# Gated delta rule in blocks of 128 tokens instead of 64, inside a two-layer encoder kernel

## The chip, the cores and the metric

One core of one Trainium2 chip runs the whole program. The metric is the device time of one execution in microseconds (us). Three runs of the kernel before took 2283.44, 2287.17 and 2287.83 us (median 2287.17).

## What is computed

Two encoder layers on a 256 x 2048 input, in float32. Layer 0 is a mixer (half A: gated delta rule, 8 heads of 128; half B: a spatial gating MLP), layer 1 a convolution module, and each layer ends with a squared-ReLU MLP. The change is in half A alone, the gated delta rule. Cut to what matters:

```python
g = jnp.cumsum(g, axis=-1)                       # within each chunk
decay = jnp.exp(jnp.where(tri, g[..., :, None] - g[..., None, :], -jnp.inf))
a = jnp.where(strict, jnp.einsum("bhnid,bhnjd->bhnij", k_beta, k) * decay, 0.0) + eye
sol = triangular_solve(a, [v_beta, k_beta * exp(g)])   # u and w
attn = jnp.einsum("bhnid,bhnjd->bhnij", q, k) * decay
q_dec, k_tail, g_last = q * exp(g), k * exp(g_end - g), exp(g_end)
# scan over chunks, state starts at zero
v_new = u_c - w_c @ state
o_c = qd_c @ state + attn_c @ v_new
state = state * gl_c + kt_c.T @ v_new
```

The reference cuts the 256 tokens into chunks of 64. The result is the same, up to rounding, for any chunk length: the chunk length is only a way to order the work.

## The kernel before, in words

**Main stream.** Weights come in chunks of 1 MB (`raw`, SP queue, L224), are split into a high part by ACT (`high_part`, L278) and a low part by DVE (`low_part`, L579), and PE multiplies. In layer 0's projections PE works by `narrow_group` (L992): one group G is 16 steps, called quarters here (`advance(st, 16 * G + 2 * i + k)`, L1014), of 12 matmuls each (L1005, L1007, L1009). Four halves of two quarters are buffered (`SPLIT = 4`).

**Side streams.** The mixer's work is written as Python generators for PE, ACT and DVE, woven by hand into the main stream. A generator yields the number of the quarter at which its next step is due. PE calls them after each quarter's 12 matmuls, so a step is put into PE's program at the end of its quarter. ACT and DVE call them once per two quarters (`side_work`, L289 and L590), right after the high or the low part that becomes possible when PE has finished the odd quarter before: work due at an even quarter or the odd one behind it is done in the same call. All three engines run in program order, so a wait in a side step also holds up the main stream behind it.

**Mixer A** (PE L1119, ACT L386, DVE L721) works on four blocks b = 2 * hh + m, of four heads (hh) and 128 tokens (m) each. Block b starts at quarter 59 + 33 * b (`BLOCK_START`, `BLOCK_TIME`), so blocks 0 and 2 start at an odd quarter, 1 and 3 at an even one. The offsets in a block are in `AT` (L35): `tok` transposes q, k, v; `gb` the decays; `feat` and `attn` the products of keys and queries; then the inverse of the unit triangular matrix C by doubling. Level lev of `LEVELS = 5` is: PE y = C * T (L1156), DVE masks it into Z (L767), PE Z * U and U * Z (L1161, L1163), DVE copies U (L770), ACT copies T (L415). One level takes two quarters; the last one leaves out U * Z. The 128-token block holds two chunks of 64, so the inverse is block diagonal. Then w (L1167) and, for each chunk cc, a step v (L1174, L1175) and a step s (L1180, L1181 and the new state L1183) with a state update on DVE (L778, L781). The head norm follows (ACT L426, L428, DVE L784 to L787), then a transpose on PE at offset `o` (L1187) and the gate (L792, L796).

**Mixer B** (DVE L799, PE L1189) has four parts at quarters 144, 160, 176 and 192; its PE steps are L1200 and L1206. After the last block of A, POOL loads x again (2 MB, L258), which ACT (L461) and DVE (L842) wait for at the first group of the output projection.

A float32 product of one head (128 x 128) is two matmul entries in the trace, a transpose is one.

Of the kernel before, what the change touches and what calls it, by code (L numbers as in the profile page):

```python
# [34 lines left out]
AT = {"tok": 0, "gb": 8, "feat": 10, "attn": 12, "t_prod": 14, "levels": 15, "w": 25, "chunks": 26, "o": 31}  # L35
# [6 lines left out]
LEVELS = 5  # L42


CONSTS = ["ident", "ones", "upto", "chunk", "fill", "strict", "lev0t"] + [f"lev{i}" for i in range(1, LEVELS + 1)]

# [17 lines left out]
def build(nc, xt, wts, w_ba, consts, params, conv_w, dw, rows, w_s, out):  # L64
    with ExitStack() as ctx:
# [34 lines left out]
        def const(name):  # L100
            return ct[:, CONSTS.index(name), :]

# [16 lines left out]
        def all_heads(ap):  # L119
# [30 lines left out]
            "tok", "tok_sq", "ss", "root", "normed", "q_decayed", "lg", "gb", "elast", "kb_copy", "decay_in", "decay",  # L150
# [18 lines left out]
        for later, first in (("sq_k", "knT"), ("sq_q", "kbT"), ("C", "kn"), ("U", "qn"), ("T", "kb"), ("Z", "knT"),  # L169
                             ("wT", "kbT"), ("v_new", "qnT"), ("state_d", "decay_s"), ("o_sq", "decay"), ("o_n", "kd"),  # L170
                             ("gate_out", "kt")):
            buf[later] = buf[first]
# [4 lines left out]
        elast = small[:, 0:4].rearrange("p a m h -> p (a m h)")[:, 0:8].rearrange("p (h c) -> p h c", c=2)  # L177
# [89 lines left out]
        def _(act):  # L267
# [118 lines left out]
            def mixer_a():  # L386
                for b in range(4):
# [13 lines left out]
                    nc.scalar.activation(elast, bank(4)[:, :, C - 1::C], ACT.Exp).then_inc(s["elast"], 1)  # L401
# [6 lines left out]
                    copy(buf["qdT"], bank(5)).then_inc(s["feat_act"], 1)  # L408
# [7 lines left out]
                    yield start + AT["w"] + 1  # L416
                    act.wait_ge(s["w_prod"], b + 1)
                    nc.scalar.activation(buf["wT"], bank(6), ACT.Copy, scale=-1.0).then_inc(s["w_copy"], 1)
                    for cc in range(2):
                        R = slice(C * cc, C * cc + C)  # L420
                        yield start + AT["chunks"] + 2 * cc + 1
                        act.wait_ge(s["v_prod"], 2 * b + cc + 1)
                        copy(buf["v_new"][R], bank(6)[R]).then_inc(s["v_copy"], 1)
                    yield start + AT["chunks"] + 4
                    act.wait_ge(s["s_prod"], 2 * b + 2)
# [138 lines left out]
        def _(dve):  # L564
# [156 lines left out]
            def mixer_a():  # L721
                for b in range(4):
# [21 lines left out]
                    tt(buf["qd"], buf["qn"], per_head(eg), ALU.mult).then_inc(s["q_decayed"], 1)  # L744
                    tt(buf["kt"], buf["kn"], per_head(et), ALU.mult)

                    yield start + AT["gb"] + 1
                    dve.wait_ge(s["elast"], b + 1)
# [3 lines left out]
                    dve.wait_ge(s["normed"], b + 1)  # L752
                    tt(buf["kd"], buf["kb"], per_head(eg), ALU.mult)
# [10 lines left out]
                    for lev in range(1, LEVELS + 1):  # L764
                        yield start + AT["levels"] + 2 * lev - 1
                        dve.wait_ge(s["y_prod"], LEVELS * b + lev)
                        tt(buf["Z"], bank(6), all_heads(const(f"lev{lev}")), ALU.mult).then_inc(s["z"], 1)  # L767
                        yield start + AT["levels"] + 2 * lev
                        dve.wait_ge(s["ut_prod"], LEVELS * b + lev)
                        nc.vector.tensor_copy(buf["U"], bank(4)).then_inc(s["u_copy"], 1)  # L770
                    if m == 0:
                        if b:
                            dve.wait_ge(s["state"], 5 * hh)
                        nc.vector.memset(buf["state"], 0.0).then_inc(s["state"], 1)
                    for cc in range(2):
                        if m == 0 or cc == 1:
                            dve.wait_ge(s["state"], 5 * hh + 2 * m + cc + 1)
                        link(tt(buf["state_d"], buf["state"], elast[:, :, cc].unsqueeze(2).to_broadcast([P, HH, P]), ALU.mult))  # L778
                        yield start + AT["chunks"] + 2 * cc + 2
                        dve.wait_ge(s["s_prod"], 2 * b + cc + 1)  # L780
                        tt(buf["state"], bank(5), buf["state_d"], ALU.add).then_inc(s["state"], 1)  # L781

# [206 lines left out]
        def _(pe):  # L989
# [108 lines left out]
            def decay_products():  # L1098

                yield GATES_START + 14  # L1100
                pe.wait_ge(s["g"], 1)
                mm(ps[:, 6, 0:16], const("upto"), gates[:, 1].rearrange("p m h -> p (m h)"), start=True, stop=True)
                mm(ps[:, 6, 16:32], const("chunk"), gates[:, 1].rearrange("p m h -> p (m h)"), start=True,
                   stop=True).then_inc(s["gc_prod"], 1)
# [13 lines left out]

            def mixer_a():  # L1119
                for b in range(4):  # L1120
# [4 lines left out]
                    if b:  # L1125
                        pe.wait_ge(s["gated"], b)
                        pe.wait_ge(s["state"], 5 * ((b - 1) // 2) + 2 * ((b - 1) % 2) + 3)
                    else:
                        pe.wait_ge(s["g"], 2)
# [12 lines left out]
                    transposes(5, lambda h: buf["qd"][:, h, :])  # L1142
                    products(6, buf["knT"], buf["kbT"]).then_inc(s["feat"], 1)
                    yield start + AT["attn"]
                    pe.wait_ge(s["feat_act"], 2 * b + 2)
# [138 lines left out]
def tables():  # L1284
# [3 lines left out]
    same = i[:, None] // C == i[None, :] // C  # L1288
    upto = same & (i[:, None] <= i[None, :])
    t = {"ident": np.eye(P), "ones": np.ones((P, P)), "upto": upto, "chunk": same,  # L1290
# [72 lines left out]
```

## Time and profile before

| | before |
|---|---|
| median of 3 runs | 2287.17 us |
| the profiled execution, its own time | 2285.45 us |
| its span, first to last instruction | 2283.5 us |
| PE busy | 2198.2 us, 14110 matmuls |
| DVE busy | 1562.1 us, 1809 instructions |
| ACT busy | 972.6 us, 1042 instructions |
| mean granted TensorE clock | 0.989 |

The span is 1.95 us shorter than the execution's own time. Matmuls are pipelined: the duration of one is about 0.28 us while the next starts 0.11 us behind it, so the time of a step is read from the starts. The mixer A work lies between 118 and 455 us of the span.

### The profile page before, as it was taken

Reading aid. Unit: us, or ns where it says so; the run is one execution under the profiler, and the core shown is the slowest. Engines: PE = TensorE matmul, PEld = TensorE weight load, DVE = VectorE, ACT = ScalarE, POOL = GpSimd, SP = SyncE. Lnnn points to the kernel's source line nnn. Section 1 sums busy time; section 2 is a strip of 40 time slices with the busy share of each in tenths; the row PEclk is TensorE's granted clock in tenths of the full one; section 3 lists DMA queues with packets and bytes.
Section 4 is the critical chain, followed back from the end, with each engine's and each line's share of the span. In section 5 each row is a group of like instructions: output and inputs, shape, how many; then the busy total and the mean of one; then the engine's idle time right before and its main releaser. Section 6 shows DMA issues by size and latency. Waiting matters only on the chain.

```text
span 2283.5 us, 36015 instructions
## 1 busy us (share of the span) xinstructions
PE 2198.2 (96%) x14110; PEld 2023.7 (89%) x14110; DVE 1562.1 (68%) x1809; ACT 972.6 (43%) x1042; POOL 11.5 (1%) x25
## 2 busy tenths in 40 slices
PE   7999999889999999999999999899999999999996
PEld 7988898889999999999999888788899999999995
DVE  8676567467765765765674999977665665665765
ACT  4544344344444544544442100155444444444553
POOL 0000000000000000000000000000000000000000
PEclk9999999999999999999999999999999999999998
DMA  6432233255555555555554444244555555555553
GB/s 226 178 112 91 98 123 121 84 193 185 202 204 202 198 193 211 197 198 197 203 201 148 151 158 153 76 163 167 203 199 198 192 206 200 201 202 202 199 192 123
DMA packets 55864, 396.84 MB, mean 174 GB/s; under 512 B 6497, under 2 KB 6881, under 8 KB 8545
## 3 DMA queue, kind: packets, MB, share of 16 engines
q1 hardware_dynamic: 54288, 389.32, 47.0%
q0 software_dynamic: 1488, 6.29, 1.0%
q8 instruction: 63, 1.03, 0.2%
q14 instruction: 25, 0.20, 0.0%
HBM read 393.49 MB, written 2.10 MB: 173 GB/s over the span
## 4 chain that ended last, share of the span: by engine, by line
PE 77%; DVE 14%; issue 4%; ACT 3%; DMA 2%; DVEq 0%; ACTq 0%; SPq 0%; POOL 0%
PE ps L1030 40%; PE ps L1032 20%; DVE work L925 4%; PE ps L1057 4%; DVE wlo L579 3%; PE ps L1005 3%; PE ps L1007 3%; PE ps L1009 3%; PE ps L1116 2%; DMA raw<-in_wts 1%; ACT whi L278 1%; DVE sq_part L619 1%; PE ps L1181 1%; PE ps L1180 1%; DVE work L686 0%
## 5 line engine op out<-in xcount | busy, mean ns | idle before, releaser
L579 DVE TENSOR_TENSOR wlo<-raw,whi 128x1024 fp32r<-128x1024 f32 x672 | 817.3, 1224 | 493.4 <-ACT whi L278 479.6
L278 ACT ACTIVATE whi<-raw 128x1024 fp32r<-128x1024 f32 x672 | 705.9, 1057 | 714.3 <-PE ps L1032 362.2
L1030 PE MATMUL ps<-hid,whi 128*128 128x512 f32 x2304 | 755.7, 382 | 5.8 <-DVE hid L958 3.3
L1030 PE MATMUL ps<-xg,whi 128*128 128x512 f32 x2048 | 672.0, 382 | 7.1 <-ACT sq_part L323 4.6
L1032 PE MATMUL ps<-hid,wlo 128*128 128x256 f32 x2304 | 628.0, 273 | 0.0
L1032 PE MATMUL ps<-xg,wlo 128*128 128x256 f32 x2048 | 558.2, 273 | 0.0
L1030 PEld LDWEIGHTS ps<-hid,whi 128*128 128x128 f32 x2304 | 435.4, 189 | 67.8 <-issue 3.9
L1032 PEld LDWEIGHTS ps<-hid,wlo 128*128 128x128 f32 x2304 | 442.4, 192 | 0.0
L1030 PEld LDWEIGHTS ps<-xg,whi 128*128 128x128 f32 x2048 | 387.1, 189 | 62.2 <-ACT sq_part L323 5.2
L1032 PEld LDWEIGHTS ps<-xg,wlo 128*128 128x128 f32 x2048 | 393.2, 192 | 0.0
L1005 PE MATMUL ps<-xg,whi 128*128 128x256 f32 x768 | 223.3, 291 | 11.1 <-DVE wlo L579 11.1
L1057 PE MATMUL ps<-work,raw 128*128 128x256 f32 x1024 | 221.5, 379 | 0.0
L1057 PEld LDWEIGHTS ps<-work,raw 128*128 128x128 f32 x1024 | 194.5, 190 | 26.4
L1007 PE MATMUL ps<-xg,whi 128*128 128x256 f32 x768 | 214.7, 280 | 0.0
L1009 PE MATMUL ps<-xg,wlo 128*128 128x256 f32 x768 | 214.3, 279 | 0.0
L925 DVE SCALAR_TENSOR_TENSOR work<-work,dwt 128x256 f32<-128x256 f32 (+1 forms) x492 | 195.5, 480 | 1.0 <-DVE work L908 0.9
L597 DVE TENSOR_TENSOR total<-ps,cross 128x1024 f32<-128x1024 f32 x68 | 98.8, 1453 | 100.3 <-ACT cross L271 97.2
L1005 PEld LDWEIGHTS ps<-xg,whi 128*128 128x128 f32 x768 | 150.8, 196 | 13.6 <-issue 12.7
L1007 PEld LDWEIGHTS ps<-xg,whi 128*128 128x128 f32 x768 | 151.0, 197 | 0.0
L1009 PEld LDWEIGHTS ps<-xg,wlo 128*128 128x128 f32 x768 | 150.9, 196 | 0.0
L271 ACT ACTIVATE cross<-ps 128x1024 f32<-128x1024 f32 x64 | 65.5, 1023 | 112.0 <-PE ps L1032 112.0
L505 ACT ACTIVATE total<-total,pt 128x256 f32<-128x256 f32 x16 | 7.3, 500 | 172.5 <-DVE total L902 172.5
(203 smaller groups left out, 1470.5 us busy)
## 6 DMA issues: line engine op xcount, KB each, us to landing
raw<-in_wts SPq DMA_DIRECT2D x368, 1024.0 KB, 4.8
x<-in_xt SPq DMA_DIRECT2D x4, 512.0 KB, 7.8
x<-in_xt POOLq DMA_DIRECT2D x1, 2048.0 KB, 9.7
out_t<-work POOLq DMA_DIRECT2D x4, 512.0 KB, 3.3
work<-in_rows POOLq DMA_DIRECT2D x12, 128.0 KB, 3.8
ct<-in_consts SPq DMA_DIRECT2D x1, 768.0 KB, 6.3
work<-in_w_s POOLq DMA_DIRECT2D x4, 128.0 KB, 4.3
dwt<-in_dw SPq DMA_DIRECT2D x1, 248.0 KB, 5.0
```

Of the source, the lines that this page charges most:

```text
L271: return nc.scalar.activation(dst, src, ACT.Copy)
L278: nc.scalar.activation(whi[:, i % SPLIT].rearrange("p a b -> p (a b)"), raw[:, r, HALF * (i % 2):HALF * (i % 2) + HALF], ACT.Copy).then_in ...
L579: tt(wlo[:, i % SPLIT].rearrange("p a b -> p (a b)"), raw[:, i // 2 % RAW, HALF * (i % 2):HALF * (i % 2) + HALF], whi[:, i % SPLIT].rearra ...
L597: tt(halves(total[:]), in_order(ps[:, 4 * par:4 * par + 4, 0:T]), in_order(cross[:]), ALU.add).then_inc(banks_free, 1)
L925: ins = stt(acc[t], src, w, acc[t], ALU.mult, ALU.add)
L1005: mm(dst, whi[:, r, k, cols], woven(operand[:, kt, 0, :]), start=(kt == 0 and n % 2 == 0), stop=False, skip_group_check=True)
L1007: mm(dst, whi[:, r, k, cols], woven(operand[:, kt, 1, :]), start=False, stop=False, skip_group_check=True)
L1009: ins = mm(dst, wlo[:, r, k, cols], woven(operand[:, kt, 0, :]), start=False, stop=(kt == KT - 1), skip_group_check=True)
L1030: mm(ps[:, 4 * par + n, :], whi[:, r, k, cols], woven_parts(operand[:, kt]), start=(kt == 0), stop=False)
L1032: ins = mm(ps[:, 4 * par + n, T:2 * T], wlo[:, r, k, cols], woven(operand[:, kt, 0, :]), start=False, stop=(kt == KT - 1))
L1057: ins = mm(ps[:, 4 * par + n, 0:T], raw[:, r, CH_N * k + P * n:CH_N * k + P * n + P], xf[:, kt, :], start=(kt == 0), stop=(kt == KT - 1))
L1116: ins = mm(bank(b)[:, h, :], left[:, h, :], right[:, h, :], start=True, stop=True)
```

## The change

The block of 128 tokens is one chunk. The inverse gets one more level (6, constant `lev6` in the place of `chunk`), due two quarters later each. The state before the first block (m = 0) is zero: with one chunk per block nothing is multiplied with it, so for m = 0 `qd`, its transpose, `kd`, w and both products with the state are left out, and the new state is a copy. For m = 1 `kt`, the state product and the state update are left out, since no block follows. The masks `upto`, `fill` and `strict` cover 128 tokens, and the sum over the chunk uses `ones`.

```diff
-AT = {"tok": 0, "gb": 8, "feat": 10, "attn": 12, "t_prod": 14, "levels": 15, "w": 25, "chunks": 26, "o": 31}
+AT = {"tok": 0, "gb": 8, "feat": 10, "attn": 12, "t_prod": 14, "levels": 15, "w": 27, "v": 28, "s": 29, "o": 31}
-LEVELS = 5
+LEVELS = 6
...
 # ACT
                     act.wait_ge(s["gb"], b + 1)
-                    nc.scalar.activation(elast, bank(4)[:, :, C - 1::C], ACT.Exp).then_inc(s["elast"], 1)
                     copy(buf["kbT"], bank(6)).then_inc(s["kb_copy"], 1)
...
-                    copy(buf["qdT"], bank(5)).then_inc(s["feat_act"], 1)
+                    if m:
+                        copy(buf["qdT"], bank(5)).then_inc(s["feat_act"], 1)
...
-                    act.wait_ge(s["w_prod"], b + 1)
-                    nc.scalar.activation(buf["wT"], bank(6), ACT.Copy, scale=-1.0).then_inc(s["w_copy"], 1)
-                    for cc in range(2):
-                        R = slice(C * cc, C * cc + C)
-                        yield start + AT["chunks"] + 2 * cc + 1
-                        act.wait_ge(s["v_prod"], 2 * b + cc + 1)
-                        copy(buf["v_new"][R], bank(6)[R]).then_inc(s["v_copy"], 1)
-                    yield start + AT["chunks"] + 4
-                    act.wait_ge(s["s_prod"], 2 * b + 2)
+                    if m:
+                        yield start + AT["w"] + 1
+                        act.wait_ge(s["w_prod"], hh + 1)
+                        nc.scalar.activation(buf["wT"], bank(5), ACT.Copy, scale=-1.0).then_inc(s["w_copy"], 1)
+                    yield start + AT["v"] + 1
+                    act.wait_ge(s["v_prod"], b + 1)
+                    copy(buf["v_new"], bank(6)).then_inc(s["v_copy"], 1)
+                    yield start + AT["s"] + 1
+                    act.wait_ge(s["s_prod"], b + 1)
...
 # DVE
-                    tt(buf["qd"], buf["qn"], per_head(eg), ALU.mult).then_inc(s["q_decayed"], 1)
-                    tt(buf["kt"], buf["kn"], per_head(et), ALU.mult)
+                    if m:
+                        tt(buf["qd"], buf["qn"], per_head(eg), ALU.mult).then_inc(s["q_decayed"], 1)
+                    else:
+                        tt(buf["kt"], buf["kn"], per_head(et), ALU.mult)
...
-                    dve.wait_ge(s["elast"], b + 1)
+                    dve.wait_ge(s["gb"], b + 1)
...
-                    dve.wait_ge(s["normed"], b + 1)
-                    tt(buf["kd"], buf["kb"], per_head(eg), ALU.mult)
+                    if m:
+                        dve.wait_ge(s["normed"], b + 1)
+                        tt(buf["kd"], buf["kb"], per_head(eg), ALU.mult)
...
+                    yield start + AT["s"] + 1
                     if m == 0:
-                        if b:
-                            dve.wait_ge(s["state"], 5 * hh)
-                        nc.vector.memset(buf["state"], 0.0).then_inc(s["state"], 1)
-                    for cc in range(2):
-                        if m == 0 or cc == 1:
-                            dve.wait_ge(s["state"], 5 * hh + 2 * m + cc + 1)
-                        link(tt(buf["state_d"], buf["state"], elast[:, :, cc].unsqueeze(2).to_broadcast([P, HH, P]), ALU.mult))
-                        yield start + AT["chunks"] + 2 * cc + 2
-                        dve.wait_ge(s["s_prod"], 2 * b + cc + 1)
-                        tt(buf["state"], bank(5), buf["state_d"], ALU.add).then_inc(s["state"], 1)
+                        dve.wait_ge(s["s_prod"], b + 1)
+                        nc.vector.tensor_copy(buf["state"], bank(5)).then_inc(s["state"], 1)
...
 # PE
+            def sums(b, left, right, step):
+                for h in range(HH):
+                    ins = mm(bank(b)[:, h, :], left[:, h, :], right[:, h, :], start=(step == 0 and h == 0),
+                             stop=(step == 1), skip_group_check=True)
+                return ins
...
-                    transposes(5, lambda h: buf["qd"][:, h, :])
+                    if m:
+                        transposes(5, lambda h: buf["qd"][:, h, :])
...
-                    products(6, buf["kd"], buf["U"]).then_inc(s["w_prod"], 1)
-                    for cc in range(2):
-                        R = slice(C * cc, C * cc + C)
-                        yield start + AT["chunks"] + 2 * cc
-                        pe.wait_ge(s["w_copy"], b + 1)
-                        pe.wait_ge(s["state"], 5 * hh + 2 * m + cc + 1)
-                        for h in range(HH):
-                            mm(bank(6)[R, h, :], buf["U"][:, h, R], buf["vb"][:, h, :], start=True, stop=False)
-                            ins = mm(bank(6)[R, h, :], buf["wT"][:, h, R], buf["state"][:, h, :], start=False, stop=True)
-                        ins.then_inc(s["v_prod"], 1)
-                        yield start + AT["chunks"] + 2 * cc + 1
-                        pe.wait_ge(s["v_copy"], 2 * b + cc + 1)
-                        for h in range(HH):
-                            mm(bank(4)[R, h, :], buf["qdT"][:, h, R], buf["state"][:, h, :], start=True, stop=False)
-                            mm(bank(4)[R, h, :], buf["attnT"][R, h, R], buf["v_new"][R, h, :], start=False, stop=True)
-                        for h in range(HH):
-                            ins = mm(bank(5)[:, h, :], buf["kt"][R, h, :], buf["v_new"][R, h, :], start=True, stop=True)
-                        ins.then_inc(s["s_prod"], 1)
+                    if m:
+                        products(5, buf["kd"], buf["U"]).then_inc(s["w_prod"], 1)
+                        pe.wait_ge(s["state"], hh + 1)
+                        sums(6, buf["U"], buf["vb"], 0)
+                        sums(4, buf["qdT"], buf["state"], 0)
+                        yield start + AT["v"]
+                        pe.wait_ge(s["w_copy"], hh + 1)
+                        sums(6, buf["wT"], buf["state"], 1).then_inc(s["v_prod"], 1)
+                    else:
+                        products(6, buf["U"], buf["vb"]).then_inc(s["v_prod"], 1)
+                    yield start + AT["s"]
+                    pe.wait_ge(s["v_copy"], b + 1)
+                    if m:
+                        ins = sums(4, buf["attnT"], buf["v_new"], 1)
+                    else:
+                        products(4, buf["attnT"], buf["v_new"])
+                        ins = products(5, buf["kt"], buf["v_new"])
+                    ins.then_inc(s["s_prod"], 1)
...
-    same = i[:, None] // C == i[None, :] // C
-    upto = same & (i[:, None] <= i[None, :])
+    upto = i[:, None] <= i[None, :]
```

## Rows read from the trace of the kernel before

**Rows 1.** The page: its first line, and the chain that ended last, by engine.

```profile
span 2283.5 us, 36015 instructions
...
PE 77%; DVE 14%; issue 4%; ACT 3%; DMA 2%; DVEq 0%; ACTq 0%; SPq 0%; POOL 0%
```

**Rows 2.** Windows by stage: length, busy us (x) of each engine, PEclk, DMA, GB/s.

```profile
118.00:455.10 337.10, 311.79 (x2511) 288.12 (x2510) 213.85 (x304) 133.77 (x173) 6.51 (x12) 0.97 0.30 105
...
555.00:2283.50 1728.50, 1688.93 (x9900) 1538.84 (x9898) 1195.07 (x1327) 728.39 (x751) 2.14 (x4) 0.99 0.51 184
```

**Rows 3.** Waits of PE, 118 to 455.1: us in total, times, longest.

```profile
PE ps L1116 <- DVE work L767: 11.6, 10, 2.4
...
PE ps L1111 <- DVE work L751: 3.5, 3, 1.9
...
PE ps L1180 <- ACT work L271: 0.9, 1, 0.9
```

**Rows 4.** Window over eight quarters of the main stream alone.

```profile
366.27:377.07 10.80, 10.80 (x99) 10.80 (x98) 9.73 (x14) 8.33 (x12) 2.12 (x4) 1.00 0.45 130
```

**Rows 5.** Timeline of PE, block 2, last levels and w: start, length, [idle before].

```profile
327.86 1.13 PE L1116 MATMUL ps<-x_space 128*128 128x128 f32 x8
330.17 1.06 PE L1116 MATMUL ps<-x_space,work 128*128 128x128 f32 x8
331.06 1.06 PE L1116 MATMUL ps<-work,x_space 128*128 128x128 f32 x8
333.49 1.13 PE L1116 MATMUL ps<-x_space 128*128 128x128 f32 x8
...
339.03 1.16 PE L1116 MATMUL ps<-x_space 128*128 128x128 f32 x8 [0.84 <-DVE x_space L770]
```

**Rows 6.** Timeline of PE, block 1, two levels.

```profile
246.63 1.06 PE L1116 MATMUL ps<-x_space 128*128 128x128 f32 x8
249.94 1.16 PE L1116 MATMUL ps<-x_space,work 128*128 128x128 f32 x8 [0.91 <-DVE work L767]
...
253.17 1.06 PE L1116 MATMUL ps<-x_space 128*128 128x128 f32 x8
```

**Rows 7.** Windows: v and s of a chunk of block 2; last s of block 0; behind it.

```profile
341.80:343.72 1.92, 1.92 (x18) 1.72 (x16) 1.12 (x2) 1.06 (x1) 0.00 (x0) 1.00 0.00 0
345.22:349.22 4.00, 4.00 (x26) 2.48 (x24) 0.57 (x1) 1.38 (x2) 0.00 (x0) 1.00 0.70 264
...
183.06:189.25 6.19, 5.28 (x26) 3.36 (x24) 1.23 (x1) 1.00 (x2) 0.00 (x0) 0.80 0.45 169
189.25:194.07 4.82, 4.82 (x25) 4.82 (x25) 2.89 (x5) 3.23 (x4) 0.00 (x0) 0.55 0.00 0
```

**Rows 8.** Timeline of ACT, then DVE, block 2 beside its chunk steps.

```profile
342.06 1.06 ACT L278 ACTIVATE whi<-raw 128x1024 fp32r<-128x1024 f32 x1 [1.24 <-PE ps L1009]
343.89 0.59 ACT L271 ACTIVATE work<-ps 64x512 f32<-64x512 f32 x1 [0.77 <-PE ps L1175]
...
352.16 1.23 DVE L579 TENSOR_TENSOR wlo<-raw,whi 128x1024 fp32r<-128x1024 f32 x1 [1.34 <-ACT whi L278]
...
354.96 0.69 DVE L820 TENSOR_TENSOR work<-work 128x512 f32<-128x512 f32 x1
```

**Rows 9.** Timeline of all engines, end of block 1.

```profile
277.57 0.69 DVE L781 TENSOR_TENSOR work<-ps,work 128x512 f32<-128x512 f32 x1 [1.53 <-PE ps L1183]
...
280.78 0.66 PE L1111 MATMUL ps<-ct,x_space 128*128 128x128 f32 x4 [0.37 <-DVE x_space L787]
```

**Rows 10.** Groups by line from 200 us on: DVE's decayed query.

```profile
L744 DVE TENSOR_TENSOR x_space<-x_space,gates 128x512 f32<-128x512 f32 x3 | 2.1, 684 | 0.0
```

**Rows 11.** Timelines of POOL, ACT and PE behind the last block.

```profile
460.31 0.54 POOL L258 DMA_DIRECT2D x<-in_xt  x1 [2.81 <-DVE hid L796]
...
471.73 2.02 ACT L278 ACTIVATE whi<-raw 128x1024 fp32r<-128x1024 f32 x2 [7.12 <-DMA raw<-in_wts]
...
482.53 2.07 PE L1206 MATMUL ps<-work 128*128 128x128 f32 x8 [6.64 <-DVE work L820]
```

More of the change, by code:

```diff
@@ L41 @@
 QKVZ_AT = [0, 8, 16, 24, 4, 12, 20, 28]
-LEVELS = 5
-CONSTS = ["ident", "ones", "upto", "chunk", "fill", "strict", "lev0t"] + [f"lev{i}" for i in range(1, LEVELS + 1)]
+LEVELS = 6
+CONSTS = ["ident", "ones", "upto", "fill", "strict", "lev0t"] + [f"lev{i}" for i in range(1, LEVELS + 1)]
 PARAMS, _at = {}, 0
@@ L148, in build @@
             "qkvz_raw", "qkvz_ready", "uv_ready",
-            "tok", "tok_sq", "ss", "root", "normed", "q_decayed", "lg", "gb", "elast", "kb_copy", "decay_in", "decay",
+            "tok", "tok_sq", "ss", "root", "normed", "q_decayed", "lg", "gb", "kb_copy", "decay_in", "decay",
             "feat_dve", "feat", "feat_act", "attn", "attn_copy", "inv0", "t_prod",
@@ L169, in build @@
         for later, first in (("sq_k", "knT"), ("sq_q", "kbT"), ("C", "kn"), ("U", "qn"), ("T", "kb"), ("Z", "knT"),
-                             ("wT", "kbT"), ("v_new", "qnT"), ("state_d", "decay_s"), ("o_sq", "decay"), ("o_n", "kd"),
+                             ("wT", "kbT"), ("v_new", "qnT"), ("o_sq", "decay"), ("o_n", "kd"),
                              ("gate_out", "kt")):
@@ L176, in build @@
         ln_g2, ln_b2, b_s2, w_s2 = (acts[:, 16 + i, :].rearrange("p (g c) -> p g c", g=2) for i in range(4))
-        elast = small[:, 0:4].rearrange("p a m h -> p (a m h)")[:, 0:8].rearrange("p (h c) -> p h c", c=2)
         flat_small = small[:].rearrange("p a m h -> p (a m h)")
@@ L415, in mixer_a @@
                         copy(buf["T"], bank(5)).then_inc(s["t_copy"], 1)
-                    yield start + AT["w"] + 1
-                    act.wait_ge(s["w_prod"], b + 1)
-                    nc.scalar.activation(buf["wT"], bank(6), ACT.Copy, scale=-1.0).then_inc(s["w_copy"], 1)
-                    for cc in range(2):
-                        R = slice(C * cc, C * cc + C)
-                        yield start + AT["chunks"] + 2 * cc + 1
-                        act.wait_ge(s["v_prod"], 2 * b + cc + 1)
-                        copy(buf["v_new"][R], bank(6)[R]).then_inc(s["v_copy"], 1)
-                    yield start + AT["chunks"] + 4
-                    act.wait_ge(s["s_prod"], 2 * b + 2)
+                    if m:
[7 more added lines that the diff above has]
+                    act.wait_ge(s["s_prod"], b + 1)
                     nc.scalar.activation(buf["o_sq"], bank(4), ACT.Square).then_inc(s["o_sq"], 1)
@@ L1102, in decay_products @@
                 mm(ps[:, 6, 0:16], const("upto"), gates[:, 1].rearrange("p m h -> p (m h)"), start=True, stop=True)
-                mm(ps[:, 6, 16:32], const("chunk"), gates[:, 1].rearrange("p m h -> p (m h)"), start=True,
+                mm(ps[:, 6, 16:32], const("ones"), gates[:, 1].rearrange("p m h -> p (m h)"), start=True,
                    stop=True).then_inc(s["gc_prod"], 1)
@@ L1126, in mixer_a @@
                         pe.wait_ge(s["gated"], b)
-                        pe.wait_ge(s["state"], 5 * ((b - 1) // 2) + 2 * ((b - 1) % 2) + 3)
+                        pe.wait_ge(s["state"], (b + 1) // 2)
                     else:
@@ L1141, in mixer_a @@
                     transposes(4, lambda h: buf["qn"][:, h, :])
-                    transposes(5, lambda h: buf["qd"][:, h, :])
+                    if m:
+                        transposes(5, lambda h: buf["qd"][:, h, :])
                     products(6, buf["knT"], buf["kbT"]).then_inc(s["feat"], 1)
                     yield start + AT["attn"]
-                    pe.wait_ge(s["feat_act"], 2 * b + 2)
+                    pe.wait_ge(s["feat_act"], 3 * hh + 2 * m + 1)
                     products(4, buf["knT"], buf["qnT"]).then_inc(s["attn"], 1)
@@ L1287, in tables @@
     i = np.arange(P)
-    same = i[:, None] // C == i[None, :] // C
-    upto = same & (i[:, None] <= i[None, :])
-    t = {"ident": np.eye(P), "ones": np.ones((P, P)), "upto": upto, "chunk": same,
+    upto = i[:, None] <= i[None, :]
+    t = {"ident": np.eye(P), "ones": np.ones((P, P)), "upto": upto,
          "fill": np.where(upto, 3e38, -3e38), "strict": upto & (i[:, None] < i[None, :])}
```

## The prediction

> **What bounds the kernel.** I read the page first: the chain that ended last runs 77% of its time through PE [rows 1]. Then the windows by stage. The change touches only the stretch from 118 to 455 us, where the side work of mixer A lies; there PE is busy 311.8 of 337.1 us, DVE 213.9 and ACT 133.8, and the DMA engines 0.30 [rows 2]. So this stretch is PE's own program, plus some 25 us in which PE stands. The waits of PE say where: 11.6 us of them before the second product of a level, for DVE's masking (L767), 3.5 us before `feat` (L751), 0.9 us once for an ACT copy before a step s [rows 3]. The reader is to see two things: what PE issues costs its full time, since nothing else is late for long, and what ACT and DVE do costs only where PE stands for it. So I count PE entries, then ask of each removed or added ACT and DVE step whether PE waits for it.
>
> **Units.** Eight quarters of the main stream alone took 10.80 us, so a quarter is 1.35 us and one matmul 0.112 us [rows 4]. Eight entries (one product for four heads) start 0.89 us ahead of the next eight [rows 5]; I take 0.90.
>
> **Removed: the chunk steps.** In block 2 a step v (16 entries) takes 1.92 us and a step s (24 entries) 4.00 us, measured between main-stream quarters [rows 7]. The second chunk repeats the pattern. That is 11.8 us a block, and the same in blocks 1 and 3: 35.5 us. In block 0 three of the four steps are alike (7.8 us); the last takes 6.19 us, at a granted clock of 0.80, and the 24 main-stream matmuls behind it take 4.82 us in place of 2.70, at 0.55, that is mostly at 1.2 GHz instead of 2.4 [rows 7]. I count all of it as gone: 7.8 + 6.2 + 2.1 = 16.1 us. Together 51.6 us.
>
> The 24 entries of a step s take 0.167 us each, more than the 0.112 us of full-width entries [rows 4, 7], although each uses only half of the array's rows or columns. The Trainium skill (TensorEngine Tiling (Array Packing), Overview and Performance Considerations) says that independent 64-wide tiles can run side by side, up to twice as fast, which speaks against widening them. By that rule the removed steps would be worth about half and the total below would shrink to some 3 us. The rows show no such overlap, so the sum goes by the rows.
>
> **Removed: small things on PE.** For m = 0 four transposes of `qd` go (4 x 0.11, twice: 0.9 us), and w is replaced one for one by the product U * vb in the same slot, so it counts nothing, and the wait before that slot (0.84 us in block 2 [rows 5]) stays.
>
> **Added: one level.** Level 5 becomes a full level, and level 6 is the one without U * Z, so a block gains one full level. In block 2 (odd start) a level repeats after 333.49 - 327.86 = 5.63 us [rows 5]; less its two quarters (2.70) it costs 2.93 us. In block 1 (even start) it is 253.17 - 246.63 = 6.54 us, with PE standing 0.91 us for DVE [rows 6]: 3.84 us. The reason for the difference is that in even blocks the DVE call does its low part first and then the mask PE waits for. Twice each: 13.5 us. Bounds: without a stall 2.7 us (24 entries), and with the longest of those waits, 2.4 us [rows 3], 5.3 us; I take the one of the row; the ten waits average 1.2 us [rows 3], so it is rather low than high.
>
> **Added: the new last steps.** For m = 0: s has 16 entries, 1.8 us, twice: 3.6. For m = 1: U * vb and qd * state join w's slot (1.8), v is 8 entries (0.9), s is 8 (0.9): 3.6, twice: 7.2. All are full-width products like those of the levels, whose price I take; at the 0.167 us an entry of the old s they would be 16 in place of 10.8 us, the upper bound.
>
> **Added: waits.** (a) m = 0, before s: ACT's copy of v_new falls into the call of the same even quarter in which PE issues s. A high part starts 0.26 us after PE's odd quarter (342.06 against 341.80), takes 1.06, and the copy 0.59 [rows 7, 8], so it is done after some 1.95 us; PE's quarter takes 1.35. PE stands 0.6 us, twice: 1.2. Queued behind it on ACT is only the next high part, which is buffered halves ahead. The 0.9 us that PE stood here in block 0 [rows 3] is in the 16.1 above. (b) Before `o`: from DVE's first step behind s to the transposes the norm chain took 280.78 - 277.57 = 3.2 us in block 1, some 3.5 us with the 0.26 us between PE's end and the next engine's start, and two quarters cover 2.7 [rows 9]; PE stood 0.37 us by the row. In block 0 the slow clock covered it; now PE stands about 0.55 us. In block 2 mixer B's normalisation on DVE ends 3.5 us after the call's low part began (355.65 less 352.16 [rows 8]), and s now ends before that, so the chain starts late: 1.1 us. Together 1.65 us. For m = 1 the first ACT copy of the chain (wT) is covered by the 1.8 us of products added in front of a full quarter, and v_new's copy by the quarter behind it, as before. The state copy on DVE for m = 0 takes the place of the add L781 (0.69 us) beside ACT's square, so the chain is not longer [rows 9].
>
> **Gained: earlier `feat`.** Each block has one DVE operation of 0.68 us less ahead of the decay rows (L744 or L745 [rows 10]); where PE waited for L751 (3.5 us over three blocks [rows 3]) this can give back up to 0.68 each. Bounds 0 and 2 us; I take 1.0, since another wait may follow. The other ACT and DVE operations that go (state updates, memset, `kd`, `elast`, one of two v_new copies) and the level's added ones that PE doesn't wait for cost nothing: DVE is busy 63% of the stretch and ACT 40%. The constants stay 12 tiles, so no load changes. The other semaphores only count differently.
>
> **The sum.** Gone: 51.6 + 0.9 + 1.0 = 53.5. Added: 13.5 + 3.6 + 7.2 + 1.2 + 1.65 = 27.2. Net 26.3 us. The profiled execution took 2285.45 us (span 2283.5 plus 1.95), so it would take 2259.1; the median of the three runs lies 1.7 us above it, which gives 2287.17 - 26.3 = 2260.9 us.
>
> **What stays.** Behind the last block POOL loads x again at 460.31, beside weight loads; ACT then waits 7.1 us for a weight chunk and PE 6.6 us at L1206 [rows 11]. All of this hangs on quarter numbers that the change leaves alone (`o` at 31, mixer B), so it moves earlier as a whole. It could shrink or grow by a few us. The remaining 1728 us [rows 2] don't see the change.
>
> **Rivals.**
> Forecast, 72%: 2256 to 2266.
> (1) The slow clock of block 0 is not removed, only moved, or another stretch joins. Those rows cost 1.1 us in the step (6.19 less 4.00 less the 0.9 wait) and 2.1 behind it, 3.3 in all [rows 7]. For it: the sixth level adds a wait to each even block. Against it: the sparse 64-wide steps with their gaps are what PE did before the clock fell, and they are gone. Gain 23: 2264; with one more stretch 20: 2267. 14%. The Trainium skill (TensorE: Matmul & The Clock Gate, Part 1) says that the slow state is the default and that activity releases it; by that rule the denser steps would rather lose slow stretches, which is the forecast.
> (2) The added chain is dearer: each of the waits I set at 0.5 to 1.1 us, some eight of them, is that of the longest one seen, 2.4 us [rows 3]; 8 x 1.6 = 13 us more: 2274. For it: block 3 runs beside mixer B. Against: that is the longest of ten, whose mean is 1.2 us. 8%.
> (3) The chain is cheaper or slow stretches beside block 3 go too: 2252 to 2256. 3%.
> (4) Slower than before: PE's clock. If the denser waits of the levels keep PE at 1.2 GHz in the mixer stretch, 24 matmuls cost 2.1 us more each [rows 7], so the 26 us are eaten up after 13 such pieces, some 60 us of time at the low clock, and at twice that the kernel is 26 us slower (2313). For it: block 3 has waits of 2.4 us. Against: over the whole stretch the clock is 0.97 even now [rows 2]. 2%.
> (5) The change doesn't act: the waits are ordered so that the removed PE time only covered ACT and DVE, and the time stays near 2287. The busy shares [rows 2] speak against it. 1%.
>
> **Range.** The range 2254 to 2269 takes in the forecast and case 1. Faster by over 0.2% (4.6 us, about what a measurement of this kernel can tell from no change): forecast and cases 1 to 3, 97%. Within 0.2%: 1%. Slower: 2%.
>
> **What the profile after would show.** The mixer stretch some 26 us shorter and all behind it as it was. PE's matmul entries 14110 - 136 = 13974: 320 of the chunk steps, 16 of w and 8 transposes go, 96 of the levels and 112 of the new steps come. DVE 1795 instructions. The wait for L767 twelve times, near 13 us. A wait of 0.6 us for ACT before s in blocks 0 and 2, and one for L787 before `o` in block 0 and 2. No clock below 1.00 between 160 and 195 us. The wait at L1206 behind the last block near 6.6 us. I am wrong if PE stands between the last level and `o` by much more than 2 us a block, or if the clock falls in new places.

## The result, and the profile after

| | before | after |
|---|---|---|
| median | 2285.31 us (4 runs) | 2259.60 us (4 runs, 2258.40 to 2260.48) |
| ratio to before | | 0.9893, 95% interval 0.9881 to 0.9906 |
| the profiled execution, its own time / span | 2285.45 / 2283.5 us | 2260.48 / 2258.7 us |
| PE matmul entries | 14110 | 13974 |
| DVE / ACT instructions | 1809 / 1042 | 1795 / 1034 |

The kernel became 25.7 us faster (95% interval 21.5 to 27.2 us); 26.3 were forecast. Its median of 2259.60 us stands against the forecast of 2260.9 and the range of 2254 to 2269. First the page of the kernel after: its span and the chain that ended last, by engine, as in [rows 1].

```profile
span 2258.7 us, 35712 instructions
...
PE 75%; DVE 15%; issue 4%; ACT 3%; DMA 2%; DVEq 0%; ACTq 0%; SPq 0%; POOL 0%
```

Nothing else has become the bound. The windows by stage of the kernel after (length, busy us (x entries) of PE, weight loads, DVE, ACT, POOL, then clock, DMA share, GB/s) answer to [rows 2]:

```profile
118.00:428.80 310.80, 282.54 (x2403) 272.94 (x2402) 205.42 (x293) 132.15 (x168) 8.07 (x15) 0.99 0.33 114
...
530.00:2258.70 1728.70, 1689.21 (x9883) 1538.55 (x9882) 1193.20 (x1326) 727.53 (x749) 2.15 (x4) 0.99 0.51 184
```

The stretch from 118 us to the end of mixer A is 310.8 us long; that of the kernel before to its matching end (457.9) was 339.9. So some 29 us went there, more than the whole kernel gained. In these two stretches PE is busy for 282.5 us where it was 314.6, and stands for 28 us where it stood for 25. So what PE issued shrank by 32 us, and its waits took 3 of them back. Its waits in this stretch (us in total, times, longest; the lines have moved, L768 is the mask that was L767) answer to [rows 3]:

```profile
PE ps L1109 <- DVE work L768: 13.4, 12, 2.4
...
PE ps L1104 <- DVE work L751: 2.9, 3, 1.3
PE ps L1104 <- DVE x_space L780: 2.1, 3, 0.8
...
PE ps L1109 <- ACT work L270: 1.6, 3, 0.9
```

The reader should see twelve waits for the mask instead of ten (two more even levels), and the head norm (L780) as a wait before `o`. The timeline of PE at the end of block 2 (start, length, [idle before]) stands against [rows 5, 7]:

```profile
318.21 1.13 PE L1109 MATMUL ps<-x_space 128*128 128x128 f32 x8
...
323.84 1.13 PE L1109 MATMUL ps<-x_space 128*128 128x128 f32 x8
...
329.82 1.16 PE L1109 MATMUL ps<-x_space 128*128 128x128 f32 x8 [0.84 <-DVE x_space L771]
334.01 1.16 PE L1109 MATMUL ps<-work 128*128 128x128 f32 x8 [0.35 <-ACT work L270]
335.01 1.06 PE L1109 MATMUL ps<-work,x_space 128*128 128x128 f32 x8
339.51 0.66 PE L1104 MATMUL ps<-ct,x_space 128*128 128x128 f32 x4 [0.77 <-DVE x_space L780]
```

The y of levels 5 and 6 (318.21, 323.84) lie 5.63 us apart, the period of before to the hundredth; then U * vb in w's slot with the same 0.84 us wait, s as two products 1.0 us apart, and the transposes of `o`. The state products have no row here, since m = 0.

Behind the last block the reload of x and the wait at L1206 moved as a whole (answers to [rows 11]; POOL, then PE):

```profile
432.19 0.54 POOL L257 DMA_DIRECT2D x<-in_xt  x1 [2.79 <-DVE hid L789]
...
454.61 2.08 PE L1206 MATMUL ps<-work 128*128 128x128 f32 x8 [6.83 <-DVE work L813]
```

There a new wait of 0.6 us stands ahead of the last full quarter (446.17; by the starts of the matmuls it costs 0.8 us), and the one at L1206 is 0.2 us longer.

### The profile page after: what moved, and what is told of

It reads as the page before. It is cut to its first block, busy times and chain, and to the rows that moved or that the text cites. A ratio compares the mean times of both kernels' runs of the same rounds, so it can differ in the third digit from the quotient of the medians.

```text
span 2258.7 us, 35712 instructions
## 1 busy us (share of the span) xinstructions
PE 2169.3 (96%) x13974; PEld 2007.9 (89%) x13974; DVE 1552.5 (69%) x1795; ACT 969.8 (43%) x1034; POOL 11.5 (1%) x25
## 4 chain that ended last, share of the span: by engine, by line
PE 75%; DVE 15%; issue 4%; ACT 3%; DMA 2%; DVEq 0%; ACTq 0%; SPq 0%; POOL 0%
PE ps L1023 40%; PE ps L1025 20%; DVE work L918 4%; DVE wlo L577 4%; PE ps L1050 4%; PE ps L1109 3%; PE ps L998 3%; PE ps L1002 3%; PE ps L1000 2%; DMA raw<-in_wts 2%; ACT whi L277 2%; DVE sq_part L617 1%; DVE work L684 0%; PE ps L1104 0%; DVE work L768 0%
## 5 line engine op out<-in xcount | busy, mean ns | idle before, releaser
L998 PE MATMUL ps<-xg,whi 128*128 128x256 f32 x768 | 221.6, 289 | 11.6 <-DVE wlo L577 11.6
```

Source lines behind the costliest of these rows:

```text
L998: mm(dst, whi[:, r, k, cols], woven(operand[:, kt, 0, :]), start=(kt == 0 and n % 2 == 0), stop=False, skip_group_check=True)
```

## The experiments

What was expected, a theory and a rival to it, stands ahead of each result. Each is compared with the kernel before run on the same chip; "to after" is the difference of the two gains (after: 25.7 us), positive where the run is slower than after. The interval of a gain reaches 2 to 4 us to either side, so a difference to after of 3 or 4 us is not clear of chance by itself; there the traces have to say what acted.

| run | median us | ratio to before (95%) | gain us | to after |
|---|---|---|---|---|
| state kept | 2262.66 | 0.9902 (0.9886 to 0.9919) | 22.5 | +3.2 |
| zero state alone, on before | 2278.67 | 0.9975 (0.9966 to 0.9985) | 6.5 | |
| five levels | 2244.81 | 0.9824 (0.9807 to 0.9840) | 40.3 | -14.6 |
| odd starts | 2251.53 | 0.9857 (0.9840 to 0.9873) | 33.6 | -7.9 |
| grouped s, on before | 2278.68 | 0.9976 (0.9967 to 0.9986) | 5.3 | |
| even starts | 2269.60 | 0.9942 (0.9927 to 0.9957) | 14.4 | +11.3 |
| early copy | 2259.40 | 0.9893 (0.9879 to 0.9907) | 24.6 | +1.1 |
| starts, copy and o | 2253.89 | 0.9872 (0.9856 to 0.9887) | 30.1 | -4.4 |
| levels earlier | 2248.76 | 0.9837 (0.9823 to 0.9851) | 37.3 | -11.6 |
| levels later | 2253.30 | 0.9861 (0.9844 to 0.9878) | 32.7 | -7.0 |

**The zero state kept.** In the changed kernel, for every m:

```diff
-                    if m:
-                        transposes(5, lambda h: buf["qd"][:, h, :])
+                    transposes(5, lambda h: buf["qd"][:, h, :])
...
+                    if m == 0:
+                        nc.vector.memset(buf["state"], 0.0).then_inc(s["state"], 1)
...
+                    products(5, buf["kd"], buf["U"]).then_inc(s["w_prod"], 1)
+                    pe.wait_ge(s["state"], 2 * hh + m + 1)
+                    sums(6, buf["U"], buf["vb"], 0)
+                    sums(4, buf["qdT"], buf["state"], 0)
+                    yield start + AT["v"]
+                    pe.wait_ge(s["w_copy"], b + 1)
+                    sums(6, buf["wT"], buf["state"], 1).then_inc(s["v_prod"], 1)
```

> The changed kernel (blocks of 128, six levels), but the zero first state is computed with: for m = 0 as well qd, its transpose, kd, w and the two products with a state that is set to zero. Theory (PE's entries at 0.112 us each plus the waits of PE make the time): per m = 0 block 4 transposes (0.45 us) and 24 more entries (2.7 us) come, and the wait of 0.6 us before s goes, so 2.5 us twice, about 5 us slower than the changed kernel, near 2265 us; the longer blocks alone then bring some 21 us of the 26. Rival (the zero state is the main part of the gain): 13 us or more slower than the changed kernel, above 2273 us.

3.2 us slower than after: nearer the theory's 5 than the rival's 13, though the two intervals overlap. In the profiles the stretch from block 0's first transposes to the output projection is 325.6 us long, where after's first has 321.9. The longer blocks alone bring 22.5 of the 25.7 us. The waits for ACT before s are gone here, as expected: of the three waits "L1109 <- ACT work" one (0.9 us, another place) is left.

**The zero state alone.** In the kernel before:

```diff
+                            first = m == 0 and cc == 0
+                            ins = mm(bank(6)[R, h, :], buf["U"][:, h, R], buf["vb"][:, h, :], start=True, stop=first)
+                            if not first:
+                                ins = mm(bank(6)[R, h, :], buf["wT"][:, h, R], buf["state"][:, h, :], start=False, stop=True)
...
+                            if not first:
+                                mm(bank(4)[R, h, :], buf["qdT"][:, h, R], buf["state"][:, h, :], start=True, stop=False)
+                            mm(bank(4)[R, h, :], buf["attnT"][R, h, R], buf["v_new"][R, h, :], start=first, stop=True)
```

> The kernel before (blocks of 64, five levels), with the two products with the zero state of the first chunk left out on PE and nothing else. Theory: in blocks 0 and 2 the first step v falls from 1.92 to about 1.1 us and the first step s from 4.00 to about 2.1 us, so 5.5 us faster than the kernel before (0.998). Rival (the steps only cover ACT and DVE): within 1 us of the kernel before.

6.5 us faster, where 5.5 were expected, and the interval (2 to 8 us) leaves out the rival's 1 us. The windows of this kernel over block 2's first v and first s show both steps at the expected size (1.92 and 4.00 before, [rows 7]):

```profile
336.96:338.04 1.08, 1.08 (x10) 0.85 (x8) 0.55 (x1) 0.82 (x1) 0.00 (x0) 1.00 0.00 0
339.51:341.67 2.16, 2.16 (x18) 1.81 (x16) 0.87 (x3) 1.38 (x2) 0.00 (x0) 1.00 0.41 80
```

That is 2.7 us a block, 5.4 us in all: what PE doesn't issue there, the time gives back in full. The step s lost 8 entries, worth 0.9 us at 0.112 each, but became 1.84 us shorter: the rest should be the changes of shape, tried by themselves below.

**One level less.**

```diff
-LEVELS = 6
+LEVELS = 5
```

The inverse stays unfinished in this kernel. The constants stay 12 tiles.

> The changed kernel without level 6 (the inverse is not finished, so this part of the computation is left out); the two quarters of level 6 stay empty. Theory: levels cost 2.93 us in blocks 0 and 2 and 3.84 us in blocks 1 and 3, together 13.5 us, and the wait of about 1.1 us before w in blocks 0 and 2 goes too: 15 to 16 us faster than the changed kernel, near 2244 us. Rival (the level hides in waits that are there anyway): less than 8 us faster.

14.6 us faster than after, near the theory's 15 to 16. The profile shows a term that the theory didn't have: with w's wait gone, PE waits longer for ACT's copies (2.9 us in three waits, up to 1.7, where after had 1.6).

**Odd starts.**

```diff
-GATES_START, BLOCK_START, BLOCK_TIME = 32, 59, 33
+GATES_START, STARTS = 32, [59, 91, 125, 157]
-                    start = BLOCK_START + BLOCK_TIME * b
+                    start = STARTS[b]
```

> The changed kernel with the blocks started at quarters 59, 91, 125 and 157 in place of 59, 92, 125 and 158, so all at odd ones. Theory (PE waits for the mask in blocks 1 and 3 because at an even start the DVE call does its low part between PE's y and the mask): the level's period in blocks 1 and 3 falls from 6.5 to some 5.65 us, 4 to 6 us a block, together 9 to 11 us faster than the changed kernel, near 2250 us. Rival (DVE is late there because of the convolution and mixer B beside it): the period stays above 6.3 us and the time within 2 us of the changed kernel.

7.9 us faster than after: below the 9 to 11, far from the rival. **Even starts** is the same edit with `[60, 92, 126, 158]`:

> The changed kernel with all blocks started at even quarters: 60, 92, 126, 158. Theory (parity decides whether PE waits for the mask): blocks 0 and 2 gain a wait of 0.9 us a level, about 4.5 us a block, less the wait before s of 0.6 us, so 7 to 9 us slower than the changed kernel, near 2267 us. Rival (load on DVE decides): within 2 us of the changed kernel.

11.3 us slower than after, above the 7 to 9. In its profile PE stands 36.7 us over the mixer stretch, 27.8 in that of after: 8.9 us more, as expected. The rest may be chance or clock, whose granted share was 0.72 from 350 to 356 us there; that was not shown. The waits of PE over the mixer stretch settle the question; first the odd starts, then the even ones:

```profile
PE ps L1104 <- DVE work L751: 5.8, 3, 2.7
PE ps L1109 <- DVE x_space L771: 5.4, 9, 1.0
```

```profile
PE ps L1109 <- DVE work L768: 26.6, 24, 2.4
```

The waits for the mask (L768) are 0 with odd starts, 13.4 us in 12 with two of four even, 26.6 us in 24 with all even. Parity decides, not the load on DVE. The timeline of PE in block 1 with odd starts shows the period: 5.70 to 5.81 us where it was 6.54 [rows 6].

```profile
227.12 1.13 PE L1109 MATMUL ps<-x_space 128*128 128x128 f32 x8 [0.31 <-DVE x_space L771]
...
232.93 1.13 PE L1109 MATMUL ps<-x_space 128*128 128x128 f32 x8 [0.21 <-DVE x_space L771]
...
238.63 1.13 PE L1109 MATMUL ps<-x_space 128*128 128x128 f32 x8
```

But the wait before `feat` (L751) doubled from 2.9 to 5.8 us, and with all starts even it was 1.3 us: the first part of a block has a parity too, and there the even start is the better one. These 2.9 us are the size by which the gain fell short.

**Step s grouped by shape**, in the kernel before:

```diff
                         for h in range(HH):
-                            mm(bank(4)[R, h, :], buf["qdT"][:, h, R], buf["state"][:, h, :], start=True, stop=False)
+                            mm(bank(4)[R, h, :], buf["qdT"][:, h, R], buf["state"][:, h, :], start=(h == 0), stop=False,
+                               skip_group_check=True)
+                        for h in range(HH):
-                            mm(bank(4)[R, h, :], buf["attnT"][R, h, R], buf["v_new"][R, h, :], start=False, stop=True)
+                            mm(bank(4)[R, h, :], buf["attnT"][R, h, R], buf["v_new"][R, h, :], start=False, stop=True,
+                               skip_group_check=True)
```

> The kernel before, with the products of step s issued by shape: first the four with the state (128 rows), then the four with v_new (64 rows). The same entries, another order. Theory (the entries of the old step s took 0.167 us each because each change of shape costs some 0.09 us more than the 0.112 us of an entry): six changes of shape fewer in each of eight steps, each step 0.5 to 1.0 us shorter, 4 to 8 us faster than the kernel before. Rival (64-wide entries are slow by themselves): within 1 us of the kernel before.

5.3 us faster with the very same entries. The window over the first s of block 2 is 3.17 us where it was 4.00 [rows 7]:

```profile
338.62:341.79 3.17, 3.17 (x26) 2.65 (x24) 0.56 (x1) 1.37 (x2) 0.00 (x0) 1.00 0.85 295
```

Eight such steps give 6.6 us by the trace; the interval of the time is 3 to 8 us. So of what the longer blocks save, some 5 to 6 us were the price of alternating between 128-row and 64-row products, which the kernel before could have had for an exchange of loops. (The edit also sets `start` for the first head alone; that this does nothing to the time was not tried by itself.)

**The early copy of v_new.**

```diff
-                    yield start + AT["v"] + 1
+                    yield start + AT["v"] + m
```

> The changed kernel with ACT's copy of v_new for m = 0 due one quarter earlier, so in the call before. Theory: the wait of PE of 0.63 us before s in blocks 0 and 2 goes; in block 2 the wait before o takes half of it back, since DVE's norms of mixer B end no earlier. About 1 us faster than the changed kernel at most, seen in the waits and not in the time. Rival (something else is late at s, such as the high part): the waits stay.

The waits before s are gone ("L1109 <- ACT work" once, 0.9 us, in place of 1.6 in three), the wait before `o` rose from 2.1 to 2.7 us, and no difference in time can be told from chance: its gain of 24.6 us lies 1.1 below after's, inside both intervals.

**All at once, with `o` later.** Starts 59, 93, 127, 161, the early copy and `"o": 32`.

> The changed kernel with all starts odd (59, 93, 127, 161), the early copy of v_new and the transposes of o one quarter later (offset 32). Theory: 9 to 11 us for the odd starts, 1 us for the copy and up to 1 us a block for o, together 11 to 14 us faster than the changed kernel, near 2247 us, if the reload of x, now two quarters later, does not make the first group of the output projection wait longer. Rival (the reload of x and the weight loads collide worse): the wait behind the last block grows from 7 to over 12 us and eats the gain of the last steps.

4.4 us faster than after, where 11 to 14 were expected, and by the medians slower than the odd starts alone (the intervals overlap). The rival did not come about either: the wait at L1206 shrank to 2.2 us. Some waits of PE grew:

```profile
PE ps L1104 <- DVE work L751: 9.3, 3, 4.1
PE ps L1109 <- DVE x_space L771: 5.1, 6, 2.7
...
PE ps L998 <- DVE hid L789: 2.4, 1, 2.4
```

In block 1 `feat` waits 3.4 us, and DVE's timeline has four operations of the convolution (1.67 us) and a low part just ahead of L751's group. In block 3 it waits 4.1 us, there behind a low part for which DVE had itself waited 1.3 us for ACT. The first output group now waits for the last block itself (L789). But all waits of PE from 118 to 460 us sum to 26.5 us here and to 29.2 us with the odd starts, so they don't make this kernel the slower one. What differs against it is the clock. The same stretch with all at once, then with the odd starts:

```profile
130.00:445.00 315.00, 294.78 (x2485) 287.19 (x2485) 207.42 (x289) 136.68 (x171) 9.16 (x17) 0.97 0.36 121
```

```profile
130.00:440.00 310.00, 291.25 (x2512) 282.93 (x2511) 204.71 (x287) 135.04 (x169) 9.16 (x17) 1.00 0.37 123
```

A granted clock of 0.97 over 315 us is of the size of the gain that is missing. That the low stretches, which lie beside waits of 2.4 to 4.1 us, come in every run of this kernel was not shown.

**Levels shifted by themselves.** With the early copy, and in blocks 1 and 3 only the part from `t_prod` on moved by a quarter (all other steps keep theirs):

```diff
                     start = BLOCK_START + BLOCK_TIME * b
+                    later = start - m
...
-                    yield start + AT["t_prod"]
+                    yield later + AT["t_prod"]
```

and so for `levels`, `w`, `v`, `s` and `o`, on all three engines.

> The changed kernel with the early copy of v_new, and in blocks 1 and 3 only the part from t_prod on (levels, w, v, s, o) one quarter earlier, so that the levels lie as in the odd blocks while the first part keeps its quarters. Theory (parity of the levels alone): the waits for the mask go (13.4 us in 12 waits), some 0.4 us a level comes back, and the wait for feat stays at 2 to 3 us and does not grow to 5.8 as with the odd starts; 8 to 11 us faster than the changed kernel, some 1 to 3 us faster than the odd starts, ratio to the kernel before near 0.984 to 0.985. Rival (the first part's end, U's first copy, is late by what the levels come earlier): a new wait of 1 us or more before t_prod in both blocks and no gain over the odd starts.

37.3 us faster than before, 11.6 more than after: the lowest median of all kernels that finish the inverse, and its interval (0.9823 to 0.9851) lies below that of after. It overlaps that of the odd starts, so the lead over them is not shown by the time. Waits of PE in its mixer stretch:

```profile
PE ps L1111 <- DVE x_space L773: 5.8, 9, 1.4
...
PE ps L1111 <- ACT x_space L270: 2.6, 1, 2.6
PE ps L1106 <- DVE work L753: 2.1, 2, 1.3
```

No wait for the mask, and `feat` (L753 here) stays at 2.1 us. The rival's new wait came once: 2.6 us for ACT's first copy of T in block 1, where after had 1.2. Shifted the other way (`start + m`):

> The same with that part one quarter later in blocks 1 and 3. Theory: the waits for the mask go just the same; the next block's first transposes then wait for the gate of block 1 (1 to 2 us once). 8 to 10 us faster than the changed kernel. Rival: as load on DVE moves with the quarters, waits of over 1 us a level stay.

7.0 us faster than after, somewhat below the 8 to 10. The mask waits are gone as well. The expected wait of the next block's first transposes did not come; a wait of 2.7 us for DVE's copy of U before w in block 1 is new.

**The two kernels once more.**

> The kernel before, profiled once more. Theory: the low clock in block 0 near 187 us belongs to what PE does there (sparse entries and waits), so it is there again. Rival: where the clock falls beside short waits differs from execution to execution, so it is gone or elsewhere, and the 3.3 us booked for it are not the change's.

The rival holds. The windows of the second profile of the kernel before, over the last step s of block 0 and the 24 matmuls behind it, against [rows 7]:

```profile
182.86:186.83 3.97, 3.97 (x24) 2.48 (x24) 0.59 (x1) 0.00 (x0) 0.00 (x0) 1.00 0.48 155
186.83:189.53 2.70, 2.70 (x25) 2.70 (x24) 1.63 (x4) 2.56 (x4) 0.00 (x0) 1.00 0.38 161
```

The same code, the same 0.9 us wait ahead of it, and a granted clock of 1.00 where it was 0.80 and 0.55. The low stretch beside block 3 (415 us) is missing too. A third difference lies in block 0, beside the wait of 3.8 to 3.9 us for DVE's L742. First the first profile of before, then the second:

```profile
121.00:129.00 8.00, 6.36 (x25) 5.22 (x26) 7.32 (x11) 3.77 (x6) 0.00 (x0) 0.57 0.33 132
```

```profile
121.00:129.00 8.00, 6.35 (x36) 5.21 (x37) 7.45 (x11) 3.78 (x6) 0.00 (x0) 0.79 0.36 130
```

By the starts of the matmuls on both sides this one cost the first profile 1.3 us more, the one near 187 us 2.6 us and the one at 415 us 1.7 us. This execution took 2281.28 us.

> The changed kernel, profiled once more. Theory: no low clock between 150 and 440 us, as in its first profile, and one near 1583 us. Rival (chance decides): a low stretch beside block 3's wait of 2.7 us, near 393 us, or none near 1583 us.

No low clock between 150 and 440 us again, so far as expected; but none near 1583 us either, which the theory had wanted. The first profile of the kernel after had one there:

```profile
1583.00:1591.00 8.00, 6.55 (x23) 5.75 (x24) 6.21 (x5) 4.27 (x5) 0.00 (x0) 0.57 0.11 35
```

It cost some 2.5 us in a stage that the change doesn't touch (the shift between the two kernels' matmuls falls from 27.3 to 24.8 us across it). The kernel before shows the same at that place: no low clock in its first profile, and a granted clock of 0.79 from 1605 to 1613 us in its second. Beside block 0's wait (121 to 129 us) the two profiles of after have 0.58 and 0.79, as those of before have 0.57 and 0.79. This execution took 2256.86 us.

## Why the prediction was right, and which term was not

By its own steps:

**Units and the level.** Right. The period of an odd level came out at 5.63 us, as costed. In blocks 1 and 3 PE still stands before the second product of every level, mostly for 0.8 to 1.1 us, and 1.8 and 2.4 us in two levels of block 3, as before. Taking level 6 away gave 14.6 us against 13.5 plus 2 for w's wait.

**The chunk steps.** Right for blocks 1 to 3. In block 0 the term was wrong: it booked 3.3 us for the low clock (2.1 behind the step and 1.1 inside) as removed by the change. The second profile of the kernel before has the step at 3.97 us and the matmuls at 2.70. So these 3.3 us belonged to that one execution, not to the code, and the rows of one profile can't tell the two apart. (The 1.1 us count from PE's restart at 184.14 us; the prediction's own subtraction, 6.19 less 4.00 less 0.9, gives 1.3.) Rival 1 was built on the same mistake. A wait beside it was off too: the second profile of before has a wait of 0.38 us before `o` in block 0, so 0.4 of the 0.55 us that the forecast added there were not new.

**The new last steps and waits.** Of the right kind, off by tenths. PE idles 0.35 us before s for ACT's copy (0.6 forecast, though PE restarts only 0.5 us late by the gap of the starts), and before `o` 0.77 us in block 2 (1.1 forecast), 0.56 in block 0 (0.55 forecast) and 0.76 in block 1, where it was 0.37 and nothing new was forecast. The step's entries are 8 per 0.89 to 1.0 us, as priced.

**`feat`.** 1.0 us forecast; the waits fell from 3.5 to 2.9 us. Blocks 1 and 3 gained 0.6 us each; block 2 lost 0.7 of it again, but only in this profile: the second one of after has no wait there, and 2.1 us in all.

**Behind the mixer.** The collision of the x reload moved as a whole, as said, and cost 1.3 us more in the first profiles and 0.9 us more in the second.

**The sum, without the clock.** The forecast's terms less the 3.3 us make 23.0 us, or 23.4 with the wait before `o` of block 0 put right. Against it stands the mixer stretch from block 0's first transposes (at 106.6 us in the kernel before, not at 118) to the first matmul of the output projection. It took 351.3 and 345.6 us in the two profiles of the kernel before, and 321.9 and 319.7 us in the two of after. The second profiles are alike in clock, each with one low stretch, near 122 us, at 0.79. They give 25.9 us; block by block 8.3, 5.0, 7.0 and 5.6 us, where the terms gave 7.3, 4.4, 5.8 and 4.4, and 1.0 for `feat`. The first profiles are alike at 122 us as well. They give 29.4 us, and 25.1 without the 4.3 us near 187 and at 415 us. Less the 1.3 and 0.9 us behind the mixer, that is 23.8 to 25.0 us. So the other terms together were 0.4 to 2 us too low. That is spread over the blocks, and why was not followed up.

The medians differ by 25.7 us, and the interval of 21.5 to 27.2 us holds all of these figures. The lowest of all 42 runs of the kernel before (2280.65) and the lowest of the five of the kernel after (2256.86) are 23.8 us apart. So that 26.3 lies within 0.6 us of the measured median is in part luck: 3.3 us of clock that the change doesn't remove stand against other terms that were too low, and against the chance in the medians. Whether the kernel before meets a low stretch more often per run is open, since most runs have no trace.

**The rivals.** The 64-wide products showed no running side by side: 24 such entries took 4.00 us and, grouped, 3.17, never less than the 2.7 of full-width ones. The tiling rule of the Trainium skill (TensorEngine Tiling (Array Packing), Overview) speaks of independent tiles. Within a step s all narrow outputs take the same 64 rows and all narrow inputs the same 64 rows, so these runs don't test the rule with tiles side by side. The same page of the Trainium skill (Tiling Modes, Key Properties) says that a change of the tiling mode drains the engine. The runs agree that a change of shape has a price and give its size, 0.83 us for six changes fewer, 0.14 each; that a drain is what costs it was not shown.

Rivals 2 and 4 rested on long waits. The longest before the second product of a level, 2.4 us, came once, as before, and the granted clock over the mixer stretch is 0.99, where it was 0.97. The slow stretch beside block 3, which rival 3 let go, is missing in both profiles of after, but in the second one of before as well. Rival 5 is excluded by the zero state alone: the time followed PE's entries.

## What to carry to other kernels

Where the busiest engine runs a program woven by hand, count its entries by their spacing and its waits by their rows; both gave the effect within some 1 us a block. Where two engines take their side work in calls of two steps, the parity of a chain's start counts beside its length: moving the levels of two blocks by one step (with the early copy) gave another 11.6 us, nearly half of what the change itself gave, and here each part of a block has its own better parity. Don't book a stretch of low clock as part of a change from one profile: take a second one.

## What the runs showed of the hardware

PE's granted clock fell, or did not, at the same place of the same code: 0.55 in one profile of the kernel before and 1.00 in the next, with the same two waits of 0.9 us ahead (at 168 and 184 us in the first). The same holds near 415 us (0.66 from 415 to 420 us in the first, beside a wait of 2.4 us) and in a later stage (0.57 in one profile of after, 1.00 in the next). Beside the long wait at L1206 (5.6 to 6.8 us) it fell in every profile that has it. The stretches that could be priced cost 1.7 to 2.6 us each, so single executions of one kernel differ by some us.

Where products of 128 x 64 and 64 x 64 shape alternate, each of two entries, the first entry behind a change starts 0.20 us after the one ahead of it and the second 0.16 us later. The same entries sorted by shape start 0.11 us apart, but for the two at a change. One sorted loop was worth 5.3 us.
